# Seven products for eight in six of the eight up projections of a second MLP

## The chip, the cores and the metric

The kernel runs on one core of a Trainium2 chip. The metric is the device time of one execution in microseconds. The engines are named as in the profile: PE (TensorE), DVE (VectorE), ACT (ScalarE), POOL (GpSimd) and SP (SyncE, which here only starts transfers).

## What is computed

Two transformer blocks follow each other on 1024 rows of width 1024, in float32. The first has a token mixer and an MLP, the second a mixer, a cross-attention and an MLP. The change concerns the second MLP, which ends the program:

```python
def squared_relu_mlp(h, mlp_w1, mlp_w2):          # h 1024x1024, w1 1024x4096, w2 4096x1024
    hdn = square(relu(einsum('bld,df->blf', h, mlp_w1)))      # up projection
    return einsum('blf,fd->bld', hdn, mlp_w2)                 # down projection
h = layer_norm(ALPHA * h + squared_relu_mlp(h, mlp_w1, mlp_w2), ln3_g, ln3_b)
```

## The kernel before

Every float32 operand of a matmul is held as two float16 parts, hi and lo, with x = hi + lo; a product is three matmuls, hi·hi, hi·lo and lo·hi, accumulated in PSUM (`gemm`, L684 to L686). A matmul has 128 rows of weights loaded and streams 512 columns.

Each MLP is cut into NF = 8 chunks of 512 hidden features. PE does the up projection of chunk 0, then for u = 0 to 6 the up projection of chunk u + 1 and the down projection of chunk u, and at the end the down projection of chunk 7. In what follows up(u) and down(u) are these. An up projection is 8 jobs (`hidden_job`), one for each 128 features and 512 rows of tokens, of 8 blocks of K times 3 matmuls: 24 each, 192 in all. A down projection is 16 jobs (`down_job`) of 4 times 3 matmuls, also 192. Jobs take the PSUM banks 0 to 3 in turn; PE waits for semaphore `evac` of the bank.

Around PE the other engines work in orders that are written out by hand, one list for each engine:

- SP loads the next half chunk of weights (1 MB) into the staging buffer `WS` (two halves) as soon as POOL has freed it.
- ACT rounds `WS` to the hi part in `WB` (L1493) and scales `WS` (L1495); `WB` has two slots, which chunks use in turn. ACT also empties the banks of an up projection into `TMP`, a ring of four (L1462), and squares there (L1741).
- POOL forms the lo part of the weights, `WB` lo = `WS` - `WB` hi (L557), then drains and raises `w_split` (L560). At the start of the second MLP it has one more task between the weights of chunk 1 and those of down(0): `residual` (L610, L612), 16 operations on the rows `R`.
- DVE turns a square in `TMP` into hi and lo of the hidden matrix `H` (`split_piece`, a CAST L2084 and a TENSOR_TENSOR L2086, one such pair is called a piece). It is this CAST that raises `evac` and so frees the bank of an up job. A down job's bank is freed when DVE has added it to `R` (`gated_add`, L2442).

DVE takes pieces and additions in one fixed order: the 8 pieces of up(1), then the 16 additions of down(0), the 8 pieces of up(2), and so on.

Of the kernel before, what the change touches and what calls it, by code (L numbers as in the profile page):

```python
# [16 lines left out]
P = 128  # L17
SEQ = 1024
D = 1024
TT = SEQ // P  # L20
KT = D // P
HALF = 512
CHUNK = 64
EPS = 1e-5
# [94 lines left out]
def program(nc, I, out, block_decay):  # L119
    ctx = ExitStack()  # L120
    with ctx:
# [34 lines left out]
        w_split = sem("w_split")  # L156
        job_done = sem("job_done")
# [35 lines left out]
        NF = 4096 // HALF  # L193

# [4 lines left out]
        def deep(c):  # L199

            return WB[:, c % 2, :, :].rearrange("p l (k n) -> p l k n", k=4)
# [19 lines left out]
        N_ENGINES = 3  # L221

# [217 lines left out]
        def _(sp):  # L440
# [42 lines left out]
            def deep_chunk(c, src):  # L483

                for hf in range(2):
                    stage(c, hf, [(WS[:, hf, :].rearrange("p (k n) -> p k n", k=2),
                                   by_k(src)[:, 2 * hf:2 * hf + 2, :])])

            def mlp_stream(c0, w1, w2):
                wide_chunk(c0, [(w1, 0, HALF)])  # L490
                with sp.Fori(0, NF - 1) as j:
                    for hf in range(2):
                        sp.wait_ge(w_stage_free, 2 * (c0 + 1) + hf + 1 + 4 * j)
                        sp.dma_start(WS[:, hf, :].rearrange("p (k n) -> p k n", k=4),
                                     by_k(w1)[:, 4 * hf:4 * hf + 4, bass.ds((j + 1) * HALF, HALF)]
                                     ).then_inc(w_loaded[hf], 16)
                    for hf in range(2):
                        sp.wait_ge(w_stage_free, 2 * (c0 + 2) + hf + 1 + 4 * j)
                        sp.dma_start(WS[:, hf, :].rearrange("p (k n) -> p k n", k=2),
                                     by_k(w2)[:, bass.ds(4 * j + 2 * hf, 2), :]).then_inc(w_loaded[hf], 16)  # L500
                deep_chunk(c0 + 2 * NF - 1, w2[(NF - 1) * HALF:NF * HALF, :])

# [15 lines left out]
            mlp_stream(C["mlp1"], w_ff1, w_ff2)  # L518
# [15 lines left out]
            mlp_stream(C["mlp2"], w1_2, w2_2)  # L534
# [13 lines left out]
        def _(pool):  # L548
# [12 lines left out]

            def gate_columns(c, n):
# [9 lines left out]
            def gate_rows(c, i=0):  # L572

                row = S[:, 12, :].rearrange("p (a n) -> p a n", a=1).to_broadcast([P, 2, D])
                for hf in range(2):
                    pool.wait_ge(w_loaded[hf], loaded_at[c] + 32 * i)
                    w = WS[:, hf, :].rearrange("p (k n) -> p k n", k=2)
                    pool.tensor_tensor(w, w, row, ALU.mult)
                    pool.drain().then_inc(w_gated, 1)

            def split_narrow(c, width):
                n = 4 * width
                for hf in range(2):
                    pool.wait_ge(w_hi, 2 * c + 1 + hf)
# [31 lines left out]
            while c < N_CHUNKS:  # L616
                if c in (C["mlp1"], C["mlp2"]):
                    for u in range(2):
                        split((c + u) % 2, 2 * (c + u) + 1, 4)
                    if c == C["mlp2"]:  # L620
                        residual(2, "wo", 0)
                    gated = c == C["mlp1"]
                    with pool.Fori(0, NF - 1 - gated) as j:
                        for u in range(2):
                            split((c + u) % 2, 2 * (c + u) + 5 + 4 * j)
                    if gated:
                        split(c % 2, 2 * (c + 14) + 1)
                        need_wide(pool, LATE_JOBS[6])
                        need_wide(pool, LATE_JOBS[7])
                        gate_rows(c + 15)  # L630
                        split((c + 15) % 2, 2 * (c + 15) + 1)
# [6 lines left out]
                else:  # L638
                    split(c % 2, 2 * c + 1, 4)
# [15 lines left out]
        used_jobs = []  # L655


        @block.tensor
        def _(pe):
# [387 lines left out]
            def mlp(c0, src, last, rest_at):  # L1047
# [8 lines left out]
                def down_job(W, j, par):  # L1056
# [2004 lines left out]
```

## Time and profile before

| | |
|---|---|
| median of 3 runs | 2814.84 us (2813.55 to 2815.96) |
| span of the profiled execution | 2814.4 us |
| second MLP in it, from its first up job to the end | about 2149 to 2814 us |

The profile is of one execution; the page gives its span, and its device time is not given apart. Start times in the rows are microseconds from the start of the span. A matmul's own duration overlaps with the next one's, so the pace of PE is read from the distance between starts.

### The profile page before, as it was taken

The numbers are of one execution on the slowest core, as the hardware profiler recorded it, in microseconds if no ns is written. First come the engines' busy times: TensorE is split into PE (matmuls) and PEld (weight loads), VectorE is DVE, ScalarE is ACT, GpSimd is POOL, SyncE is SP. The second block draws the span as 40 slices with busy tenths as digits, with TensorE's granted clock in tenths as the row PEclk, the third lists the DMA queues.
The fourth block names the chain that finished last, engine by engine and source line by source line (L and its number), as shares of the span: only waits on it lengthen the run. The fifth ranks groups of instructions, "written<-read, shape, count | busy, mean of one in ns | idle before, by whom it ended". The sixth has DMA issues, their size and how long they took to land.

```text
span 2814.4 us, 33977 instructions
## 1 busy us (share of the span) xinstructions
PE 2653.3 (94%) x13340; PEld 1368.6 (49%) x13340; DVE 1435.5 (51%) x2294; ACT 966.3 (34%) x1154; POOL 686.1 (24%) x355
## 2 busy tenths in 40 slices
PE   6999999888999999999978899888999999999998
PEld 3677766444444444444454444344544444444443
DVE  6255344565744444675675749654336622222225
ACT  3434315035223332334244353253425332332231
POOL 1212024012212212321542231126013621221222
PEclk9999999999999999999989999999999999999999
DMA  7311131202111101221021230110001111110111
GB/s 302 117 60 68 43 120 46 90 30 90 54 37 60 60 30 60 75 96 40 31 90 66 70 116 30 45 44 32 31 30 60 60 42 49 60 60 31 60 45 60
DMA packets 55590, 182.44 MB, mean 65 GB/s; under 512 B 3952, under 2 KB 4368, under 8 KB 48016
## 3 DMA queue, kind: packets, MB, share of 16 engines
q1 hardware_dynamic: 47136, 138.89, 14.5%
q10 hardware_dynamic: 8304, 41.46, 4.0%
q8 instruction: 105, 1.72, 0.3%
q14 instruction: 45, 0.37, 0.0%
HBM read 170.90 MB, written 9.45 MB: 64 GB/s over the span
## 4 chain that ended last, share of the span: by engine, by line
PE 77%; DVE 9%; ACT 4%; POOLq 3%; DVEq 3%; issue 2%; POOL 1%; DMA 1%; ACTq 1%; SPq 0%
PE PS L684 23%; PE PS L685 23%; PE PS L686 23%; POOLq L613 1%; DVE XT L2086 1%; POOLq L611 1%; PE PS L723 1%; PE PS L1426 1%; POOL WB L557 1%; DVEq L2085 1%; PE PS L1399 1%; ACT WB L1493 1%; ACT WS L1495 1%; PE PS L972 1%; DMA Hf<-in_w_ada 1%
## 5 line engine op out<-in xcount | busy, mean ns | idle before, releaser
L557 POOL TENSOR_TENSOR WB<-WS,WB 128x512 f16<-128x512 f32 (+1 forms) x264 | 488.1, 1881 | 1854.4 <-ACT WS L1495 1854.1
L684 PE MATMUL PS<-XT,WB 128*128 128x512 f16 x1568 | 597.7, 381 | 10.5 <-DVE Hf L2084 5.3
L685 PE MATMUL PS<-XT,WB 128*128 128x512 f16 x1568 | 597.8, 381 | 0.0
L686 PE MATMUL PS<-XT,WB 128*128 128x512 f16 x1568 | 597.0, 381 | 0.0
L684 PE MATMUL PS<-WB,Hf 128*128 128x512 f16 x1440 | 551.5, 383 | 21.1 <-DVE Hf L2086 5.1
L685 PE MATMUL PS<-WB,Hf 128*128 128x512 f16 x1440 | 550.7, 382 | 0.0
L686 PE MATMUL PS<-WB,Hf 128*128 128x512 f16 x1440 | 550.3, 382 | 0.0
L2084 DVE CAST Hf<-S 128x512 f16<-128x512 f32 x172 | 148.8, 865 | 490.2 <-ACT S L1741 385.5
L1493 ACT ACTIVATE WB<-WS 128x2048 f16<-128x2048 f32 (+3 forms) x118 | 212.5, 1801 | 506.3 <-PE PS L686 471.1
L2442 DVE SCALAR_TENSOR_TENSOR R<-PS,R 128x512 f32<-128x512 f32 x208 | 143.0, 691 | 258.9 <-PE PS L686 251.8
L684 PEld LDWEIGHTS PS<-XT,WB 128*128 128x128 f16 x1568 | 154.2, 98 | 196.4 <-DVE XT L2086 5.5
L686 PEld LDWEIGHTS PS<-XT,WB 128*128 128x128 f16 x1568 | 154.1, 98 | 187.1 <-issue 3.8
L685 PEld LDWEIGHTS PS<-XT,WB 128*128 128x128 f16 x1568 | 154.0, 98 | 184.4 <-issue 3.1
L684 PEld LDWEIGHTS PS<-WB,Hf 128*128 128x128 f16 x1440 | 142.1, 99 | 198.6 <-issue 13.2
L686 PEld LDWEIGHTS PS<-WB,Hf 128*128 128x128 f16 x1440 | 142.0, 99 | 173.4 <-issue 6.3
L685 PEld LDWEIGHTS PS<-WB,Hf 128*128 128x128 f16 x1440 | 142.1, 99 | 172.8 <-issue 7.8
L1462 ACT ACTIVATE S<-PS 128x512 f32<-128x512 f32 x148 | 87.6, 594 | 393.5 <-PE PS L686 368.5
L1495 ACT ACTIVATE WS<-WS 128x2048 f32<-128x2048 f32 (+3 forms) x118 | 212.0, 1797 | 0.0
L684 PE MATMUL PS<-WB,XT 128*128 128x256 f16 (+2 forms) x640 | 169.0, 273 | 3.8 <-POOLq L588 2.3
L685 PE MATMUL PS<-WB,XT 128*128 128x256 f16 (+2 forms) x640 | 168.9, 273 | 0.0
L686 PE MATMUL PS<-WB,XT 128*128 128x256 f16 (+2 forms) x640 | 168.9, 273 | 0.0
L2086 DVE TENSOR_TENSOR Hf<-S,Hf 128x512 f16<-128x512 f32 x172 | 160.0, 930 | 16.2 <-issue 0.4
(381 smaller groups left out, 2744.2 us busy)
## 6 DMA issues: line engine op xcount, KB each, us to landing
WS<-in_w_ff SPq DMA_DIRECT2D x32, 1024.0 KB, 5.1
WS<-in_mlp_w SPq DMA_DIRECT2D x32, 1024.0 KB, 5.2
WS<-in_w_mix SPq DMA_DIRECT2D x20, 1024.0 KB, 4.9
Hf<-in_w_ada ACTq DMA_DIRECT2D x12, 1024.0 KB, 5.8
Hf<-in_w_ada SPq DMA_DIRECT2D x8, 1024.0 KB, 10.9
WS<-in_w_out SPq DMA_DIRECT2D x8, 1024.0 KB, 5.1
R<-in_x SPq DMA_DIRECT2D x4, 1024.0 KB, 9.9
R<-in_x ACTq DMA_DIRECT2D x2, 2048.0 KB, 7.9
```

Of the source, the lines that this page charges most:

```text
L557: op = pool.tensor_tensor(WB[:, slot, 1, at:at + n], WS[:, hf, i * n:(i + 1) * n], WB[:, slot, 0, at:at + n], ALU.subtract)
L611: pool.drain()
L613: pool.drain().then_inc(res_ready, 1)
L684: pe.matmul(o, ah, bh, start=(first and k == 0), stop=False, skip_group_check=True)
L685: pe.matmul(o, ah, bl, start=False, stop=False, skip_group_check=True)
L686: mm = pe.matmul(o, al, bh, start=False, stop=(last and k == n - 1), skip_group_check=True)
L1462: return act.activation(TMP[:, q % 4, :], src, func, scale=scale, bias=bias)
L1493: act.activation(rank_pair(hf, 0) if n == 64 else WB[:, slot, 0, hf * n:(hf + 1) * n], WS[:, hf, 0:n], ACT.Copy, scale=W_SCALE)
L1495: act.activation(WS[:, hf, 0:n], WS[:, hf, 0:n], ACT.Copy, scale=W_SCALE).then_inc(w_hi, 1)
L2084: dve.tensor_copy(hi, TMP[:, q % 4, :]).then_inc(evac[bank], 1)
L2086: dve.tensor_tensor(lo, TMP[:, q % 4, :], hi, ALU.subtract).then_inc(piece_done, 1)
L2442: dve.scalar_tensor_tensor(r, PS[:, b, :], 1 / (W_SCALE * scale * (ALPHA if first else 1.0)), r, ALU.mult, ALU.add).then_inc(evac[b], 1)
```

## The change

`FAST` names the chunks 2 to 7 of the second MLP. For these the up projection is done in half blocks: the 1024 of K and the 512 features of a weight chunk are cut into q11, q12, q21, q22 (512 by 256 each), the 1024x1024 activations into a11, a12, a21, a22 (512 by 512), and the four blocks of the result are formed from seven products of sums and differences (`PRODUCTS`) in place of eight products. Each product is 2 groups (256 features are 2 times 128) of 4 blocks of K times 3 matmuls.

- The sums of activation blocks s1 to s4 are formed once, by DVE, in `corner_sums(j)`: a call after each of the 8 pieces of up(1). They live in `S` as hi and lo.
- The differences of weight blocks t1 to t4 are formed by POOL for every fast chunk (`form_sums`), in place in `WS`. ACT rounds each of the seven forms to hi and POOL forms each lo (`split_forms`).
- The products use banks 4 to 7. ACT copies intermediate ones to `kept`, DVE adds them (`product_sum`) into `TMP`, ACT squares, DVE splits (`split_hidden`).
- PE does six products of up(u), the first two jobs of down(u - 1), the seventh product, and the other 14 jobs.
- In both MLPs the loops of ACT, POOL, DVE and SP are written out, a down chunk is staged and split by halves of its output columns, and PE starts a down projection when the half it needs is there (`w_half`), all jobs of one half first.

The core of the diff:

```diff
 
...
+        FORM_INDEX = {"q11": 0, "q21": 1, "q22": 2, "t1": 3, "t2": 4, "t3": 5, "t4": 6}
+        FORM_HI = {"q11": 1, "q21": 2, "t1": 3, "q22": 2, "t2": 4, "t3": 5, "t4": 6}
+        QUAD_AT = {"q11": (0, 0), "t3": (0, 0), "t1": (0, 1), "q12": (0, 1), "q21": (1, 0), "t4": (1, 0),
+                   "q22": (1, 1), "t2": (1, 1)}
...
+        def form_at(m, u, form, l):
+
+            i, a = FORM_INDEX[form], fast_slot(m, u)
+            slot, i = (a, i) if i < 4 else (1 - a, i - 4)
+            return WB[:, slot, l, i * 1024:(i + 1) * 1024].rearrange("p (k n) -> p k n", k=4)
+        KEPT_UNITS = {"mlp2": (11, 12)}
+
...
+            def split_down(m, u, gated=False):
+
+                c, slot = down_chunk(m, u), down_slot(m, u)
+                for hf in range(2):
+                    pool.wait_ge(w_hi, hi_count(c) + 1 + hf)
+                    n = slice(hf * 2048, (hf + 1) * 2048)
...
+            def split_forms(m, u):
+
+                at = FAST_BASE[m] + u - 2
+
+                def form_sums(forms):
+
+                    for form in forms:
+                        out, a, b = {"t1": ("q12", "q12", "q11"), "t2": ("q22", "q22", "t1"), "t3": ("q11", "t2", "q11"),
+                                     "t4": ("q21", "q21", "t2")}[form]
+                        pool.tensor_tensor(quad_stage(out), quad_stage(a), quad_stage(b), ALU.subtract)
+                        pool.drain().then_inc(form_sum, 1)
+
+                for form in FORM_INDEX:
+                    if form == "q21":
+                        form_sums(("t1",))
+                    if form == "t1":
+                        form_sums(("t2",))
+                    if form == "t2":
+                        form_sums(("t3", "t4"))
+                    pool.wait_ge(form_hi, 6 * at + FORM_HI[form])
+                    pool.tensor_tensor(form_at(m, u, form, 1), quad_stage(form), form_at(m, u, form, 0), ALU.subtract)
+                    pool.drain().then_inc(form_lo, 1)
+                    if form in ("t3", "t4"):
...
+                        if u in FAST[m]:
+                            split_forms(m, u)
+                        elif u > 1:
...
+                def fast_product(u, i):
+
+                    at = FAST_BASE[m] + u - 2
+                    form, rows, bank = PRODUCTS[i]
+                    pe.wait_ge(form_lo, 7 * at + FORM_INDEX[form] + 1)
+                    for f in range(2):
+                        if form == "q21" and at:
+                            pe.wait_ge(up_sum, 6 * (at - 1) + 3 + f)
+                        if form == "q11" and at:
+                            pe.wait_ge(up_last, 2 * (at - 1) + 1 + f)
+                        if form == "t1":
+                            pe.wait_ge(up_kept, 6 * at + 1 + f)
+                        if form == "t2":
+                            pe.wait_ge(up_sum, 6 * at + 1 + f)
+                        if form == "q22":
+                            pe.wait_ge(up_kept, 6 * at + 3 + f)
+                        if form == "t3":
+                            pe.wait_ge(up_kept, 6 * at + 5 + f)
+                        if form == "t4":
+                            pe.wait_ge(up_sum, 6 * at + 5 + f)
+                        c = slice(f * P, (f + 1) * P)
+                        gemm(PS[:, 4 + bank + f, :], lambda k: tuple(form_at(m, u, form, l)[:, k, c] for l in range(2)),
+                             lambda k: tuple(sum_rows(m, rows, l, k) if rows in SIGN_UNITS[m] else
+                                             block_rows(rows, l, k) for l in range(2)), 4,
+                             first=form in ("q21", "q11", "t1")).then_inc(up_done, 1)
 
...
+
+                    c = up_chunk(m, u)
+                    if u in fast:
+                        if u == fast[0]:
+                            for k in range(K[0] - 4, K[0]):
+                                need_side(pe, k)
+                            pe.wait_ge(corner_sum, 4 * (1 + (m == "mlp2" and len(FAST["mlp1"]) > 0)))
...
-                    pe.wait_ge(piece_done, q0 + 8 * (u + 1))
+                    down_at[m, u - 1] = J[0]
+                    pe.wait_ge(piece_done, q0 + 8 * u)
                     for j in range(16):
-                        down_job(deep(c + 1), j, u % 2)
+                        if j % 8 == 0:
+                            need_half(u - 1, j // 8)
+                        down_job(u - 1, j % 8, j // 8)
+                        if j == 1 and u in fast:
+                            fast_product(u, 6)
                     chunk_used()
-
...
+                def up_forms(u):
+
+                    c, at = up_chunk(m, u), FAST_BASE[m] + u - 2
+                    if u == fast[0]:
+                        act.wait_ge(job_done, used_jobs[up_chunk(m, u - 1)])
+                    else:
+                        act.wait_ge(up_done, 14 * at)
+                    for hf, forms in enumerate((("q11",), ("q21", "q22"))):
+                        act.wait_ge(w_loaded[hf], loaded_at[c])
+                        for form in forms:
+                            act.activation(form_at(m, u, form, 0), quad_stage(form), ACT.Copy, scale=W_SCALE)
+                        act.drain()
+                        act.activation(WS[:, hf, :], WS[:, hf, :], ACT.Copy, scale=W_SCALE).then_inc(form_hi, 1)
+                    act.wait_ge(form_sum, 4 * at + 1)
+                    form_round(u, "t1").then_inc(form_hi, 1)
+                    act.wait_ge(job_done, down_at[m, u - 2] + 8)
+                    act.wait_ge(form_sum, 4 * at + 2)
+                    form_round(u, "t2").then_inc(form_hi, 1)
+                    act.wait_ge(form_sum, 4 * at + 3)
+                    form_round(u, "t3").then_inc(form_hi, 1)
+
+                def last_form(u):
+
+                    at = FAST_BASE[m] + u - 2
+                    act.wait_ge(job_done, down_at[m, u - 2] + 16)
+                    act.wait_ge(form_sum, 4 * at + 4)
+                    form_round(u, "t4").then_inc(form_hi, 1)
+
...
+                        act.wait_ge(up_sum, 6 * at + n + 1)
+                        act.activation(TMP[:, q % 4, :], TMP[:, q % 4, :], ACT.Relu, scale=UNSCALE * F_SCALE ** 0.5)
+                        act.drain()
+                        act.activation(TMP[:, q % 4, :], TMP[:, q % 4, :], ACT.Square).then_inc(tmp_full, 1)
+
+                    if at:
+                        act.wait_ge(up_sum, 6 * at)
+                    for f in range(2):
+                        keep(0, f, f)
+                    squared(0)
+                    round_down(u - 1, 0)
+                    keep(1, 4, 0)
+                    squared(1)
+                    keep(1, 5, 1)
+                    for f in range(2):
+                        keep(0, 6 + f, f)
+                    round_down(u - 1, 1)
+                    for n in range(2, 6):
+                        squared(n)
+                    for f in range(2):
+                        act.wait_ge(up_done, 14 * at + 13 + f)
+                        q = Q[0]
+                        to_tmp(PS[:, 6 + f, :], ACT.Relu, scale=UNSCALE * F_SCALE ** 0.5).then_inc(up_last, 1)
...
+                def product_sum(u, n):
+
+                    at, f = FAST_BASE[m] + u - 2, n % 2
+                    bank, i, job, copy = ((4, 0, 2, 1), (4, 0, 8, 5), (6, 1, 10, 3))[n // 2]
+                    if n < 2:
+                        bank = 6
+                    dve.wait_ge(up_kept, 6 * at + copy + f)
+                    dve.wait_ge(up_done, 14 * at + job + f + 1)
+                    dve.drain()
+                    dve.tensor_tensor(TMP[:, (Q[0] + n - 2 * (n >= 2)) % 4, :], PS[:, bank + f, :], kept(m, i, f),
+                                      ALU.add).then_inc(up_sum, 1)
+
+                def corner_sums(j):
+
+                    k = j // 2
+                    a11, a12, x, y = kept(m, 0, 0), kept(m, 0, 1), kept(m, 1, 0), kept(m, 1, 1)
+
+                    def joined(dst, name):
+                        dve.tensor_tensor(dst, block_rows(name, 0, k), block_rows(name, 1, k), ALU.add)
+
+                    def parts(name, x):
+                        dve.drain()
+                        dve.tensor_copy(sum_rows(m, name, 0, k), x)
+                        dve.drain()
+                        return dve.tensor_tensor(sum_rows(m, name, 1, k), x, sum_rows(m, name, 0, k), ALU.subtract)
+
+                    if j % 2 == 0:
+                        joined(x, "a21")
+                        joined(y, "a22")
+                        joined(a11, "a11")
+                        joined(a12, "a12")
+                        dve.drain()
+                        dve.tensor_tensor(y, x, y, ALU.add)
+                        dve.tensor_tensor(x, a11, x, ALU.subtract)
+                        parts("s1", y)
+                    else:
+                        parts("s3", x)
+                        dve.drain()
+                        dve.tensor_tensor(y, y, a11, ALU.subtract)
+                        dve.drain()
+                        dve.tensor_tensor(a12, a12, y, ALU.subtract)
+                        parts("s2", y)
+                        parts("s4", a12)
...
-                hidden(1, 0, None if last else s5_steps)
-                down(0, False)
+                for u in range(NF):
+                    if u in fast:
+                        for n in range(2):
+                            product_sum(u, n)
+                        for n in range(2):
+                            split_hidden(u, n)
+                        for n in range(2, 6):
+                            product_sum(u, n)
+                        for n in range(2, 6):
+                            split_hidden(u, n)
+                    elif u == 1 and fast:
+                        hidden(u, corner_sums)
+                    else:
+                        hidden(u, None if last else {0: s5_setup, 1: s5_folds, NF - 1: s5_steps}.get(u))
```

What a built program of each kernel has on an engine shows the same. On DVE, this stands at the start of the second MLP, where the pieces of up(0) end and those of up(1) follow (Hf is `H`). Before:

```order
L2084 CAST Hf<-S 128x512 [waits tmp_full]
L2086 TENSOR_TENSOR Hf<-S,Hf 128x512
L2083 REGISTER_ALU
L2084 CAST Hf<-S 128x512 [waits tmp_full]
L2086 TENSOR_TENSOR Hf<-S,Hf 128x512
```

Now, from the first piece of up(1) to the second one and the operations behind it:

```order
L2316 CAST Hf<-S 128x512 [waits tmp_full]
L2318 TENSOR_TENSOR Hf<-S,Hf 128x512
L2759 TENSOR_TENSOR S<-XT 128x512 x4
L2773 TENSOR_TENSOR S<-S 128x512
L2774 TENSOR_TENSOR S<-S 128x512
L2763 CAST S<-S 128x512
L2765 TENSOR_TENSOR S<-S 128x512
L2316 CAST Hf<-S 128x512 [waits tmp_full]
L2318 TENSOR_TENSOR Hf<-S,Hf 128x512
L2763 CAST S<-S 128x512
L2765 TENSOR_TENSOR S<-S 128x512
L2779 TENSOR_TENSOR S<-S 128x512
```

Between two pieces of up(1) there are now eight operations of `corner_sums`, 64 in all, and the additions of down(0) stand behind all of them.

On POOL, the end of `residual` is followed before by the loop over the splits:

```order
L612 TENSOR_TENSOR R<-R,S 128x1024
L623 UNCONDITIONAL_BRANCH
L623 ISA
L557 TENSOR_TENSOR WB<-WS,WB 128x2048 [waits w_hi]
```

and now by the split of down(0), all of the forms of chunk 2, and the split of down(1):

```order
L707 TENSOR_TENSOR R<-R,S 128x1024
L625 TENSOR_TENSOR WB<-WS,WB 128x2048 [waits w_hi] x2
L650 TENSOR_TENSOR WB<-WS,WB 128x1024 [waits form_hi]
L639 TENSOR_TENSOR WS<-WS 128x4x256
L650 TENSOR_TENSOR WB<-WS,WB 128x1024 [waits form_hi] x2
L639 TENSOR_TENSOR WS<-WS 128x4x256
L650 TENSOR_TENSOR WB<-WS,WB 128x1024 [waits form_hi]
L639 TENSOR_TENSOR WS<-WS 128x4x256 x2
L650 TENSOR_TENSOR WB<-WS,WB 128x1024 [waits form_hi] x3
L625 TENSOR_TENSOR WB<-WS,WB 128x2048 [waits w_hi] x2
```

A chunk's up weights thus cost POOL 11 operations of half the size in place of 2.

## Rows read from the trace of the kernel before

**Rows 1.** The page: busy time of the engines and share of the span.

```profile
PE 2653.3 (94%) x13340; PEld 1368.6 (49%) x13340; DVE 1435.5 (51%) x2294; ACT 966.3 (34%) x1154; POOL 686.1 (24%) x355
```

**Rows 2.** PE's waits from 2150 to 2815 us: us in total, times, longest.

```profile
PE PS L684 <- POOLq L560: 3.8, 1, 3.8
```

**Rows 3.** Busy us in stretches, in the page's order of engines; then granted clock, DMA.

```profile
2220.00:2240.00 20.00, 16.17 (x68) 6.95 (x68) 9.35 (x9) 8.65 (x6) 12.05 (x3) 0.91 0.55 172
2267.15:2350.03 82.88, 82.88 (x386) 37.59 (x384) 23.16 (x32) 24.21 (x24) 16.23 (x4) 1.00 0.16 51
```

**Rows 4.** Timeline of PE: start, us; end of up(1), start of down(0), up(2).

```profile
2219.59 0.38 PE L685 MATMUL PS<-XT,WB 128*128 128x512 f16 x1
2219.80 0.38 PE L686 MATMUL PS<-XT,WB 128*128 128x512 f16 x1
2224.01 0.49 PE L684 MATMUL PS<-WB,Hf 128*128 128x512 f16 x1 [3.83 <-POOLq L560]
...
2227.65 0.38 PE L684 MATMUL PS<-WB,Hf 128*128 128x512 f16 x1
...
2267.15 0.38 PE L684 MATMUL PS<-XT,WB 128*128 128x512 f16 x1
```

**Rows 5.** Timeline of DVE: pieces of up(1), from the first to the last.

```profile
2188.49 0.43 DVE L2084 CAST Hf<-S 128x512 f16<-128x512 f32 x1 [4.61 <-ACT S L1741]
2189.01 2.69 DVE L2086 TENSOR_TENSOR Hf<-S,Hf 128x512 f16<-128x512 f32 x1
2191.61 2.56 DVE L2084 CAST Hf<-S 128x512 f16<-128x512 f32 x1
2194.27 2.70 DVE L2086 TENSOR_TENSOR Hf<-S,Hf 128x512 f16<-128x512 f32 x1
...
2212.76 2.57 DVE L2084 CAST Hf<-S 128x512 f16<-128x512 f32 x1
2215.42 4.55 DVE L2086 TENSOR_TENSOR Hf<-S,Hf 128x512 f16<-128x512 f32 x1
2219.89 4.28 DVE L2084 CAST Hf<-S 128x512 f16<-128x512 f32 x1
2224.26 0.69 DVE L2086 TENSOR_TENSOR Hf<-S,Hf 128x512 f16<-128x512 f32 x1
2224.87 0.42 DVE L2084 CAST Hf<-S 128x512 f16<-128x512 f32 x1
2225.38 0.69 DVE L2086 TENSOR_TENSOR Hf<-S,Hf 128x512 f16<-128x512 f32 x1
```

**Rows 6.** Timeline of POOL in that stretch, and a split without DVE beside it.

```profile
2212.43 2.61 POOL L612 TENSOR_TENSOR R<-R,S 128x1024 f32<-128x1024 f32 x1
2215.35 8.54 POOL L557 TENSOR_TENSOR WB<-WS,WB 128x2048 f16<-128x2048 f32 x2 [0.31 <-issue]
2228.64 4.08 POOL L557 TENSOR_TENSOR WB<-WS,WB 128x2048 f16<-128x2048 f32 x1 [4.75 <-ACT WS L1495]
```

**Rows 7.** Groups of POOL by form: busy, mean ns of one, idle before.

```profile
L612 POOL TENSOR_TENSOR R<-R,S 128x1024 f32<-128x1024 f32 x24 | 59.2, 2465 | 3.5
L587 POOL TENSOR_TENSOR WB<-WS,WB 128x1024 f16<-128x1024 f32 x6 | 13.6, 2296 | 79.5 <-ACT WS L1495 79.5
```

**Rows 8.** Timeline of DVE while POOL is idle, the last three with a drain.

```profile
2121.08 0.42 DVE L2084 CAST XT<-S 128x512 f16<-128x512 f32 x1
2121.59 0.69 DVE L2086 TENSOR_TENSOR XT<-S,XT 128x512 f16<-128x512 f32 x1
2122.20 0.42 DVE L2084 CAST XT<-S 128x512 f16<-128x512 f32 x1
...
1735.89 0.69 DVE L2893 TENSOR_TENSOR S<-S 128x512 f32<-128x512 f32 x1
1736.65 0.69 DVE L2895 TENSOR_TENSOR S<-S 128x512 f32<-128x512 f32 x1
```

**Rows 9.** Timeline of ACT: a half chunk rounded and scaled, a bank emptied and squared.

```profile
2267.43 1.91 ACT L1493 ACTIVATE WB<-WS 128x2048 f16<-128x2048 f32 x1 [34.30 <-PE PS L686]
2269.24 1.89 ACT L1495 ACTIVATE WS<-WS 128x2048 f32<-128x2048 f32 x1
2277.79 0.60 ACT L1462 ACTIVATE S<-PS 128x512 f32<-128x512 f32 x1 [1.87 <-PE PS L686]
2278.45 0.63 ACT L1741 ACTIVATE S<-S 128x512 f32<-128x512 f32 x1
```

**Rows 10.** Timeline of DVE and of SP: an addition of down(0); a chunk's two transfers.

```profile
2228.50 0.69 DVE L2442 SCALAR_TENSOR_TENSOR R<-PS,R 128x512 f32<-128x512 f32 x1 [2.42 <-PE PS L686]
...
2275.48 4.39 SPq L494 DMA_DIRECT2D WS<-in_mlp_w  x2
```

More of the change, by code:

```diff
@@ L156, in program @@
         w_split = sem("w_split")
+        w_half = sem("w_half")
+        form_hi, form_lo, form_sum = sem("form_hi"), sem("form_lo"), sem("form_sum")
+        sums_in = sem("sums_in")
+        up_done, up_kept, up_sum, up_last = sem("up_done"), sem("up_kept"), sem("up_sum"), sem("up_last")
+        corner_sum = sem("corner_sum")
         job_done = sem("job_done")
@@ L1045, in _, with mlp @@
             pieces += 16
-            def mlp(c0, src, last, rest_at):
+            def mlp(m, src, last, rest_at):
+                c0, fast = C[m], FAST[m]
                 def hidden_job(W, j):
@@ L1433, in _ @@
             pieces += 16
[L1434 removed]
+            mlp("mlp2", None, True, 2)
         @block.scalar
@@ L1726, in _, with mlp, hidden @@
                       second=False)
-            def mlp(c0, name, lnw, lnb, last):
-                def hidden(extra_j, extra_q, setup=None, first=False):
+            def mlp(m, name, lnw, lnb, last):
+                c0, fast = C[m], FAST[m]
+                def hidden(setup=None, first=False):
                     for i in range(8):
@@ new lines, in round_down, with form_round @@
+                def round_down(u, hf, gated=None):
+                    c = down_chunk(m, u)
+                    if gated is not None:
+                        act.wait_ge(w_gated, gated + hf)
+                    down_free(u, hf)
+                    round_half(down_slot(m, u), hf, 2048, loaded_at[c], None)
+                def form_round(u, form):
+                    return act.activation(form_at(m, u, form, 0), quad_stage(form), ACT.Copy)
+                def up_forms(u):
[17 more added lines that the diff above has]
+                    form_round(u, "t3").then_inc(form_hi, 1)
@@ L2482, in _, with mlp, hidden @@
             J[0] += 2 * TT
-            def mlp(gate, par, last):
-                def hidden(par_, extra_q, setup=None):
+            def mlp(m, gate, par, last):
+                fast = FAST[m]
+                def hidden(u, setup=None):
                     for j in range(8):
@@ L2496, in down @@
+                def down(u, tail, between=None):
                     for j in range(16):
@@ L2512, in mlp, with between @@
-                with dve.Fori(0, 3 if last else 2) as i:
-                    for u in range(2):
-                        hidden((u + 1) % 2, 16 * i)
-                        if last and u == 0:
-                            dve.wait_ge(res_ready, 24)
-                        down(48 * i, False)
-                J[0] += 96 if last else 48
-                Q[0] += 32 if last else 16
-                hidden(1, 0, None if last else s5_steps)
-                down(0, False)
+                for u in range(NF):
+                    if u in fast:
+                        for n in range(2):
[8 more added lines that the diff above has]
+                        hidden(u, corner_sums)
+                    else:
+                        hidden(u, None if last else {0: s5_setup, 1: s5_folds, NF - 1: s5_steps}.get(u))
+                    if u == 0:
+                        continue
+                    if u == 1 and last:
+                        dve.wait_ge(res_ready, 24)
+                    def between(j):
+                        if u in fast and j in (1, 2):
+                            split_hidden(u, 5 + j)
+                    down(u - 1, False, between)
```

238 lines of the change are left out of this document (146 added, 92 removed).

## The prediction

> **What bounds the kernel now.** I read the page first: PE is busy 94% of the span, no other engine over 51% [rows 1]. Then PE's waits inside the second MLP: there is a single one, of 3.8 us, ended by POOL [rows 2]. Then stretches by time: a chunk pair (up and down) takes 82.88 us in which PE never idles, at the full granted clock [rows 3]; it holds 384 matmuls, so 0.2158 us each, which is also the distance between two starts [rows 4]. So from 2267.15 on PE sets the end, and every matmul that goes is worth 0.216 us as long as no wait appears. The start of this MLP is another matter. From 2191.6 to 2226.1 us DVE has no gap: its CASTs and TENSOR_TENSORs take 2.6 us instead of 0.42 and 0.69 [rows 5, 8], each ending just after an operation of POOL, whose `residual` runs without a pause until 2215.0 and is followed by 8.5 us of splits [rows 6]. PE does not feel this, since nothing waits closely for those pieces: DVE's last piece of up(1) ends at 2226.07 [rows 5], two us before the first addition of down(0) at 2228.50 [rows 10] has its bank.
>
> **What is removed.** A fast chunk has 7 products of 24 matmuls, 168 for 192. Six chunks save 144 matmuls: 144 x 0.2158 = **31.1 us**, at the full clock and with no new wait.
>
> **What the fast chunks add, and why it hides.** I lay out one chunk from T, the start of its first product. A group of 12 matmuls is 2.59 us, a product 5.18, the chunk 30 groups or 77.7 us. Prices: an ACT rounding or scaling of a half chunk 1.9, a bank emptied 0.60, a squaring pass 0.63 [rows 9]; 1024 columns on ACT by interpolation between 512 and 2048 about 1.0; a POOL lo part of 1024 columns 2.3, a difference in float32 2.5 [rows 7], a split of a half 4.1 [rows 6]; both transfers of a chunk 4.4 [rows 10].
> - Forms of the next chunk: ACT is through with this chunk at about T+43.4 and rounds and scales the two halves until T+50.4. POOL takes from T+46.4 eight operations, about 20 us, then t2 and t3 (ACT may round them once the first half of the down jobs is done, T+57), until T+71. PE asks for them at T+78 and later; t4 is ready at T+81 and is used at T+114.
> - Down weights: the first half of `WS` is free at T-7, loaded well before T, rounded by ACT behind the second product (T+14), split by POOL at T+18.5. PE needs it at T+31. The second is at T+34, needed at T+57.
> - Banks 4 to 7: each is copied or added (0.6 to 0.7) while PE works one product, 5.2 us, in another pair. DVE's additions read PSUM and one SBUF tensor, a kind that takes 0.69 even beside POOL (the addition at 2228.50 beside the split at 2228.64) [rows 6, 10]. The seventh product needs its sums at T+36.3, they are there at T+31.8.
> The smallest slack is thus 4.5 us. POOL is busy about 36 of 77.7 us, ACT about 45. I cost all this at nothing; if a cover is gone, a chunk pays the lateness, six times.
>
> **Halves and written-out loops.** PE now starts down(0) with POOL's first half split. It was done at about 2219.6, half of the 8.5 us [rows 6], and PE was ready at 2220.0 [rows 4]. So the 3.8 us wait would go, and the eight half-speed matmuls behind it too (2224.01 to 2227.65 for 8 matmuls and a bit; granted clock 0.91 in that stretch, that is some time at 1.2 in place of 2.4 GHz [rows 3, 4]), 1.7 us more. But a later stall comes in its place, next. The first MLP has no such wait; its engines have the same work in the same order, and I cost it at nothing.
>
> **What corner_sums costs, the term that decides.** It puts 64 DVE operations of 128x512 between the pieces of up(1). Without POOL beside them: after a TENSOR_TENSOR the next starts 0.61 us later, 0.76 with a drain between; after a CAST 0.51 [rows 8]. An even call is 3 x 0.61 + 0.76 + 0.61 + 0.76 + 0.51 + 0.61 = 5.1, an odd one 5.6. Four of each: **42.9 us**, 0.67 an operation. All of them come on top, since DVE had no gap there. While `residual` and the split of down(0) last, DVE gets one operation for each of POOL's, whatever it is; before, the thirteen of 2188.5 to 2224.3 were all of pieces, now four are and nine are sums. The total of what comes behind is the same.
>
> Then POOL comes back while DVE is still at it: ACT ends its squares of up(1) when PE has done job 7. PE's jobs 5, 6, 7 wait for DVE (they need the CASTs of pieces 1, 2, 3, at 2215.3, 2229.7 and 2236), job 7 ends near 2242, so ACT starts the forms of chunk 2 near 2243 and POOL near 2246. Eight POOL operations follow without a wait (the ninth needs eight down jobs, which don't exist yet). Against each, one DVE operation takes about 2.56 for 0.67 [rows 5]: 8 x 1.9 = **15.1 us** more. This has two ends. None blocked gives 0. More than eight can't be blocked there, so 15.1 is near the top; I take 15.1, since every operation of up(1)'s pieces behaves so wherever POOL runs [rows 5].
>
> This is where a rule of the Trainium skill speaks against the change. Its page SBUF — State Buffer, section SBUF: two separate sides, says that VectorE and GpSimd share a port pair as an exclusive lock held for the whole instruction, by a VectorE operation with two SBUF inputs or in a two-port mode against GpSimd; the other fully blocks. The trace agrees with 2.70 for 0.69 us. The rows have no operation with two float16 inputs; by the rule those of `joined` block as well.
>
> DVE would end piece 7 and its sums at 2226.07 + 42.9 + 15.1 = 2284.1. Down jobs 0 to 3 of down(0) get their banks from pieces 4 to 7, but job 4 needs the first addition, and that stands behind everything: 2284.1 + 0.17 + 0.69 = 2284.9. PE then has 12 jobs, 31.1 us, with the first eight matmuls at half speed after the stall, 1.7: up(2) starts at 2317.7. Before, 2267.15 [rows 4]. That is **+50.5 us**, in which the 3.8 + 1.7 of before are already counted as gone.
>
> **The sum.** 50.5 - 31.1 = +19.4 us: a span of 2814.4 + 19.4 = 2833.8. The profiled span lies 0.4 under the median of the runs, 2814.84, so a run should take about **2834 us**.
>
> **Rivals.**
> 1. *POOL doesn't catch DVE in its sums* (it starts later, or DVE slips several operations through a gap between two of POOL's). The 15.1 falls away: up(2) starts at 2302.6, +4.3 net, 2819 us. For it: POOL's start depends on a chain of ACT and PE that I placed only to a few us. Against it: in the 32 us of `residual` DVE never got two through [rows 5]. A partial form, half of the eight, gives 2827.
> 2. *Faster.* The sums are cheap enough for PE's lead over DVE. Job 4 of down(0) could start at 2230.4 without any stall; the change breaks even when DVE ends 19.4 us earlier than in my sum, at 2264.7 rather than 2284.1. One mechanism does it: the lock spares the sums, because operations on `XT` and `S` alone aren't blocked by POOL, in `residual` either. Then DVE does the sums, 42.9, and eight pieces at 1.12, 9.0, straight from 2188.5 and ends at 2240.4; job 4 starts at 2241.3, up(2) 32.8 later at 2274.1, 6.9 behind 2267.15, and the result is 2814.8 + 6.9 - 31.1 = 2791 (some us more for pieces that stay blocked). Against it: two-input operations on `S` and `Hf` are blocked in [rows 5], and nothing in the rows sets `XT` apart.
> 3. *The sixteen additions of hi and lo run at twice the pace*, 0.27 us less each, 4.3 in all: 2830, inside my range. They read float16 and write float32.
> 4. *The fast chunks stall too.* POOL's or ACT's chain is longer than laid out, or DVE's CASTs, held by a POOL that is now busy half the time, are late for the seventh product. At 2 us a chunk the time is 2846; if each chunk loses its whole 5.18 the time is 2865. For it: the 4.5 us of slack is small. Against it: most chains have over 12.
>
> On rival 3, the page VectorE: DVE Perf Modes of the Trainium skill, section What auto-detection actually checks, gives the double pace of a two-input operation only where every tensor is 16-bit. By that rule the sum stays at 2834; no row here has such an operation.
>
> **How the numbers follow.** A measurement of this kernel can tell about 0.2%, 5.6 us, from no change: 2809.2 to 2820.5 is "same". My forecast, with its partial forms and rival 3 (2825 to 2842): 0.70. Rival 1 in full, around 2819, falls on both sides of that bound: 0.10. Rival 2: 0.09. Rival 4: 0.11. So faster 0.10, same 0.09, slower 0.81. The range 2816 to 2846 takes in rival 1, and rival 4 in its mild form; outside stay rival 2 and the strong form of 4, under 2 in 10.
>
> **What the profile would show.** If I am right: PE waits for DVE at jobs 5 to 7 of up(1) and at jobs 1 to 4 of down(0), some 50 us in all, the last ending at about 2285; DVE busy without a gap from 2188 to 2286, with durations near 2.6 us until 2224 and again from about 2246 to 2266; up(2) starting near 2318; then six stretches of 77.7 us and PE without a wait to the end. If the eight aren't blocked, the durations between 2246 and 2266 are 0.4 to 0.7. If the lock spares the sums, DVE's operations are short before 2224 as well. If rival 4 holds, PE waits for `form_lo`, `w_half` or `up_sum` in each fast chunk. I am wrong altogether if PE has work that I don't see while DVE is at its sums, or if banks 4 to 7 tie a product to something later.

## The result, and the profile after

The changed kernel takes 2836.09 us (median of 4 runs, 2834.71 to 2837.59) against 2815.11 (4 runs, 2813.55 to 2815.96): a ratio of 1.0072, 95% interval 1.0059 to 1.0085. It is 21 us slower (17 to 24 by the interval). The forecast was 2834 us, and slower had been given 0.81. The profiled execution has a span of 2832.9 us, and its device time, 2834.71 us, is 1.8 us more.

The page of the changed kernel, busy time by engine, answers to [rows 1]:

```profile
PE 2631.5 (93%) x13196; PEld 1359.5 (48%) x13196; DVE 1519.7 (54%) x2394; ACT 1007.9 (36%) x1220; POOL 784.5 (28%) x409
```

PE has the 144 matmuls less (13340 to 13196), and still ends later. Its busy time falls by 22 us and not by the 31.1 that 144 matmuls take, since some 50 matmuls now run at half speed behind the waits shown next. The view of its waits in the second MLP (us in total, times, longest), where [rows 2] had one row of 3.8 us:

```profile
PE PS L783 <- DVE Hf L2316: 40.4, 6, 11.7
PE PS L783 <- DVE R L2674: 4.6, 1, 4.6
```

The wait for POOL is gone, and DVE is the new releaser, first with the CASTs that free up banks (L2316), at last with the first addition of down(0) (L2674). PE's timeline where the long waits end, and up(2):

```profile
2212.94 0.61 PE L783 MATMUL PS<-XT,WB 128*128 128x512 f16 x1 [9.19 <-DVE Hf L2316]
2229.03 0.61 PE L783 MATMUL PS<-XT,WB 128*128 128x512 f16 x1 [9.05 <-DVE Hf L2316]
2253.75 0.61 PE L783 MATMUL PS<-WB,Hf 128*128 128x512 f16 x1 [9.04 <-DVE Hf L2316]
2269.93 0.61 PE L783 MATMUL PS<-WB,Hf 128*128 128x512 f16 x1 [11.65 <-DVE Hf L2316]
2283.45 0.61 PE L783 MATMUL PS<-WB,Hf 128*128 128x512 f16 x1 [4.60 <-DVE R L2674]
2316.80 0.38 PE L783 MATMUL PS<-XT,WB 128*128 128x512 f16 x1
```

Up(2) starts at 2316.80 in place of 2267.15 [rows 4]: 49.65 us later. DVE's timeline shows what it did instead, over the same stretch as [rows 5]:

```profile
2187.59 0.43 DVE L2316 CAST Hf<-S 128x512 f16<-128x512 f32 x1 [4.60 <-ACT S L1885]
2188.11 2.69 DVE L2318 TENSOR_TENSOR Hf<-S,Hf 128x512 f16<-128x512 f32 x1
2190.72 8.95 DVE L2759 TENSOR_TENSOR S<-XT 128x512 f32<-128x512 f16 x4
2199.75 2.68 DVE L2773 TENSOR_TENSOR S<-S 128x512 f32<-128x512 f32 x1
...
2229.67 2.49 DVE L2759 TENSOR_TENSOR S<-XT 128x512 f32<-128x512 f16 x4
2232.24 0.69 DVE L2773 TENSOR_TENSOR S<-S 128x512 f32<-128x512 f32 x1
...
2246.45 2.19 DVE L2763 CAST S<-S 128x512 f16<-128x512 f32 x1
2248.72 2.71 DVE L2765 TENSOR_TENSOR S<-S 128x512 f16<-128x512 f32 x1
...
2281.83 0.69 DVE L2765 TENSOR_TENSOR S<-S 128x512 f16<-128x512 f32 x1
2282.70 3.04 DVE L2674 SCALAR_TENSOR_TENSOR R<-PS,R 128x512 f32<-128x512 f32 x4 [0.18 <-issue]
```

The same four additions of `joined` take 2.49 us when POOL rests and 8.95 beside `residual`. The second slow stretch, from 2246.45 on, begins with POOL's forms of chunk 2 (POOL's timeline: the first two and the last of the eight that follow each other, then the ninth):

```profile
2246.06 2.30 POOL L650 TENSOR_TENSOR WB<-WS,WB 128x1024 f16<-128x1024 f32 x1 [22.25 <-ACT WS L1924]
2248.54 2.34 POOL L639 TENSOR_TENSOR WS<-WS 128x1024 f32<-128x1024 f32 x1 [0.18 <-issue]
...
2263.68 2.57 POOL L639 TENSOR_TENSOR WS<-WS 128x1024 f32<-128x1024 f32 x1 [0.18 <-issue]
2297.42 2.13 POOL L650 TENSOR_TENSOR WB<-WS,WB 128x1024 f16<-128x1024 f32 x1 [31.17 <-ACT WB L1910]
```

And in stretches, with the columns of [rows 3]: the time of the stalls, then two of the six fast chunks.

```profile
2260.00:2280.00 20.00, 7.72 (x24) 2.74 (x24) 18.65 (x24) 0.00 (x0) 5.89 (x3) 0.66 0.00 0
2316.30:2394.00 77.70, 77.70 (x362) 35.24 (x360) 27.72 (x38) 31.12 (x35) 32.46 (x13) 1.00 0.17 55
2549.50:2627.30 77.80, 77.80 (x362) 35.31 (x361) 27.72 (x38) 31.12 (x35) 32.48 (x13) 1.00 0.17 55
```

A fast chunk takes 77.7 us at the full granted clock where a plain one took 82.88 [rows 3]. From the start of up(2) to the end of the span it is 516.1 us now (2832.9 - 2316.8) and 547.25 before (2814.4 - 2267.15). So the seven products give 31.15 us, and all of the loss lies ahead of them.

The executions differ by some us before they come to the changed part, so a second measure is of use: the time from one and the same matmul to the end of the span. I take PE's first matmul behind its last transposes (`PS<-BASE`). In both kernels 14 jobs of up projections lie between it and down(0). Up(0) itself begins two jobs earlier, at 2131.35 in the trace of before, and not at 2149 as the table of the kernel before has it. Before, and in the changed kernel:

```profile
2147.50 0.38 PE L684 MATMUL PS<-XT,WB 128*128 128x512 f16 x1
```

```profile
2146.60 0.38 PE L783 MATMUL PS<-XT,WB 128*128 128x512 f16 x1
```

From there to the end it is 666.9 us before (2814.4 - 2147.5) and 686.3 now (2832.9 - 2146.6), 19.4 us more. The table below gives the same measure for the experiments.

### The profile page after: what moved, and what is told of

The parts are those of the page before. It is cut to its first block, busy times and chain, and to the rows that moved or that the text cites. A ratio compares the mean times of both kernels' runs of the same rounds, so it can differ in the third digit from the quotient of the medians.

```text
span 2832.9 us, 33523 instructions
## 1 busy us (share of the span) xinstructions
PE 2631.5 (93%) x13196; PEld 1359.5 (48%) x13196; DVE 1519.7 (54%) x2394; ACT 1007.9 (36%) x1220; POOL 784.5 (28%) x409
## 4 chain that ended last, share of the span: by engine, by line
PE 77%; DVE 11%; ACT 4%; DVEq 3%; issue 2%; POOLq 1%; DMA 1%; ACTq 1%; POOL 0%; SPq 0%
PE PS L783 23%; PE PS L784 22%; PE PS L785 22%; PE PS L822 1%; DVE XT L2318 1%; PE PS L1567 1%; DVEq L2317 1%; DVE Hf L2318 1%; ACT WB L1634 1%; PE PS L1540 1%; DVE S L2765 1%; ACT WS L1636 1%; PE PS L1071 1%; POOLq L708 1%; DMA Hf<-in_w_ada 1%
## 5 line engine op out<-in xcount | busy, mean ns | idle before, releaser
L614 POOL TENSOR_TENSOR WB<-WS,WB 128x512 f16<-128x512 f32 (+1 forms) x220 | 308.1, 1433 | 1221.5 <-ACT WS L1636 1221.5
L783 PE MATMUL PS<-XT,WB 128*128 128x512 f16 x1328 | 508.5, 383 | 28.9 <-DVE Hf L2316 23.5
L784 PE MATMUL PS<-XT,WB 128*128 128x512 f16 x1328 | 508.2, 383 | 0.0
L785 PE MATMUL PS<-XT,WB 128*128 128x512 f16 x1328 | 507.1, 382 | 0.0
L1634 ACT ACTIVATE WB<-WS 128x2048 f16<-128x2048 f32 (+3 forms) x106 | 189.9, 1791 | 332.9 <-PE PS L785 302.0
L2674 DVE SCALAR_TENSOR_TENSOR R<-PS,R 128x512 f32<-128x512 f32 x208 | 143.0, 691 | 240.4 <-PE PS L785 231.8
L2316 DVE CAST Hf<-S 128x512 f16<-128x512 f32 x124 | 99.7, 804 | 302.1 <-ACT S L1885 196.5
L625 POOL TENSOR_TENSOR WB<-WS,WB 128x2048 f16<-128x2048 f32 x32 | 131.1, 4098 | 374.8 <-ACT WS L1636 372.7
L783 PEld LDWEIGHTS PS<-XT,WB 128*128 128x128 f16 x1328 | 130.9, 99 | 188.2 <-DVE Hf L2316 19.2
L785 PEld LDWEIGHTS PS<-XT,WB 128*128 128x128 f16 x1328 | 131.0, 99 | 159.9 <-issue 5.8
L784 PEld LDWEIGHTS PS<-XT,WB 128*128 128x128 f16 x1328 | 130.9, 99 | 156.2 <-issue 4.1
L1636 ACT ACTIVATE WS<-WS 128x2048 f32<-128x2048 f32 (+3 forms) x106 | 189.2, 1785 | 0.0
L1603 ACT ACTIVATE S<-PS 128x512 f32<-128x512 f32 x112 | 66.2, 594 | 298.4 <-PE PS L785 273.5
## 6 DMA issues: line engine op xcount, KB each, us to landing
Hf<-in_w_ada SPq DMA_DIRECT2D x8, 1024.0 KB, 10.6
```

Of the source, the lines that this page charges most:

```text
L614: op = pool.tensor_tensor(WB[:, slot, 1, at:at + n], WS[:, hf, i * n:(i + 1) * n], WB[:, slot, 0, at:at + n], ALU.subtract)
L625: pool.tensor_tensor(WB[:, slot, 1, n], WS[:, hf, :], WB[:, slot, 0, n], ALU.subtract).then_inc(w_stage_free, 1)
L783: pe.matmul(o, ah, bh, start=(first and k == 0), stop=False, skip_group_check=True)
L784: pe.matmul(o, ah, bl, start=False, stop=False, skip_group_check=True)
L785: mm = pe.matmul(o, al, bh, start=False, stop=(last and k == n - 1), skip_group_check=True)
L1603: return act.activation(TMP[:, q % 4, :], src, func, scale=scale, bias=bias)
```

## The experiments

The ratios are against the kernel before on the same chip. The kernel before ran at a median of 2816.45 us beside e1 to e4 and 2816.33 beside e5 and e6, so ratios are compared rather than times. A ratio has an interval of some us. The traces are finer, one execution each: this is the time from the matmul named above to the end of the span, against the 666.9 us of the kernel before.

| | that matmul starts | to the end | against before | expected |
|---|---|---|---|---|
| the change | 2146.60 | 686.3 | +19.4 | +19.4 |
| e1 | 2151.45 | 661.3 | -5.6 | -5.5 |
| e2 | 2149.87 | 670.2 | +3.3 | +4.4 |
| e3 | 2146.66 | 656.3 | -10.6 | -31 |
| e4 | 2150.05 | 668.7 | +1.8 | +2 |
| e5 | 2148.03 | 635.4 | -31.5 | -30.7 |
| e6 | 2152.90 | 707.9 | +41.0 | +40.4 |

For e2 and e6, whose expectations are told against the changed kernel (15 us less, 21 more), the last column adds its 19.4. The second column shows that the executions reach this matmul up to 6 us apart, whatever the version.

**e1: no fast chunk.** Only the written-out loops and the halves stay.

```diff
-        FAST = {"mlp1": range(0), "mlp2": range(2, NF)}
+        FAST = {"mlp1": range(0), "mlp2": range(0)}
```

> No fast chunk at all: what is left of the change is the written-out loops and the down weights by halves. My theory: these alone are worth the 3.8 us wait at the start of down(0) and the 1.7 us of half-speed matmuls behind it, so about 2809.5 us and PE without a wait from 2150 us on. Rival: the longer programs of ACT, DVE and POOL or the transfers with shorter rows cost something of their own, and part of the +21 us of the whole change is here: then 2815 us or more.

Measured: 2811.47 us, ratio 0.9983 (0.9973 to 0.9992), 4.8 us faster. PE has no wait from `residual` to the end; what the view lists from 2130 us on is ahead of the MLP. My theory's 5.5 us lies within the interval (2.3 to 7.6), and the trace is nearer to it: 5.6 us less from the matmul above to the end. The rival, a cost of the longer programs, falls. The 49.65 us are therefore not in this part.

**e2: POOL's forms of chunk 2 wait for the sums.**

```diff
                 at = FAST_BASE[m] + u - 2
+                if at == 0:
+                    pool.wait_ge(corner_sum, 4)
 
                 def form_sums(forms):
```

> The changed kernel, but POOL starts the forms of chunk 2 only when DVE has finished corner_sums. My theory: the eight POOL operations that ran beside the sums held eight DVE operations for about 1.9 us each; without them the sums end near 2267, up(2) starts near 2302 in place of 2316.8, and the time is 15 us lower, about 2821 us. Rival: the sums cost what they cost by their number, and DVE's long durations only name an idle time that something else sets: then up(2) starts where it did, 2836 us. Second rival: the forms now come late for the first products, and PE waits for form_lo: the gain is part of 15 us.

Measured: 2820.37 us, ratio 1.0013 (1.0004 to 1.0022). Against the 1.0072 of the change that is 16.6 us less (4.5 either way by the two intervals), where I expected 15. Its timeline of DVE behind 2246 has no long duration, and the one of POOL shows its first form after the sums:

```profile
2190.86 0.43 DVE L2318 CAST Hf<-S 128x512 f16<-128x512 f32 x1 [4.61 <-ACT S L1887]
...
2251.35 0.69 DVE L2320 TENSOR_TENSOR Hf<-S,Hf 128x512 f16<-128x512 f32 x1
2252.13 0.43 DVE L2765 CAST S<-S 128x512 f16<-128x512 f32 x1
...
2269.89 0.69 DVE L2767 TENSOR_TENSOR S<-S 128x512 f16<-128x512 f32 x1
2270.77 3.04 DVE L2676 SCALAR_TENSOR_TENSOR R<-PS,R 128x512 f32<-128x512 f32 x4 [0.18 <-issue]
```

```profile
2270.70 2.12 POOL L652 TENSOR_TENSOR WB<-WS,WB 128x1024 f16<-128x1024 f32 x1 [43.61 <-DVEq L2786]
```

Adding a wait to POOL made the kernel faster. DVE's instructions are the same in both; only what POOL did beside them differs. From the first CAST of up(1) to the last sum DVE took 79.7 us here (2270.58 - 2190.86) and 94.9 in the changed kernel (2282.52 - 2187.59): 15.2 us less. That is the part of the loss in which POOL's operations hold DVE's. The waits of PE are all for DVE, none for `form_lo`, so the second rival falls too.

**e3: five fast chunks, the sums between the additions of down(0) and down(1).** The helper functions for slots and counts are moved by one chunk as well, since FAST now begins at 3.

```diff
-        FAST = {"mlp1": range(0), "mlp2": range(2, NF)}
+        FAST = {"mlp1": range(0), "mlp2": range(3, NF)}
...
-                    elif u == 1 and fast:
-                        hidden(u, corner_sums)
...
                         if u in fast and j in (1, 2):
                             split_hidden(u, 5 + j)
+                        if last and u in (1, 2) and j % 4 == 1:
+                            corner_sums(4 * (u - 1) + j // 4)
```

> Fast chunks 3 to 7 (five), and corner_sums taken out of the pieces of up(1): one of its eight calls behind every fourth addition of down(0) and down(1), where DVE has 1.9 us free per addition. My theory: a call (5.1 to 5.6 us) and four additions (3.5) fit in the 10.4 us that PE takes for four jobs, and PE is four banks ahead, so nothing stalls: 2815.1 - 5.5 - 5 x 5.18 = 2784 us. Rival: POOL's splits, which fall into the same stretches, hold the sums so long that PE runs out of banks: some us in each of down(0) and down(1), 2790 us or more.

Measured: 2806.39 us, ratio 0.9965 (0.9951 to 0.9979): 9.9 us faster than before, not 31. My expectation missed by 21 us, on the side of its rival. PE's waits:

```profile
PE PS L785 <- DVE R L2676: 15.7, 2, 10.7
PE PS L785 <- DVEq L2786: 1.2, 1, 1.2
```

The two waits for an addition are behind the first call in each of down(0) and down(1). With the third they make 16.9 us, and the half-speed matmuls behind the two add some 3.6, which is the 21 us missed. The one in down(1), on DVE and on POOL:

```profile
2315.06 9.02 DVE L2761 TENSOR_TENSOR S<-XT 128x512 f32<-128x512 f16 x4
2324.16 2.67 DVE L2775 TENSOR_TENSOR S<-S 128x512 f32<-128x512 f32 x1
```

```profile
2315.88 2.59 POOL L641 TENSOR_TENSOR WS<-WS 128x1024 f32<-128x1024 f32 x1 [0.18 <-issue]
```

A call that I had priced at 5.1 us took 19.6 (2315.06 to 2334.6), since it ran beside POOL's forms of chunk 3, which began at 2313.57. The other calls of down(1) ran nearly all beside an idle POOL, and PE's only further wait, at the start of up(3), is the one of 1.2 us. I had made the same mistake as the change: room on DVE counted without asking what POOL does then.

**e4: six fast chunks, all sums in down(0).**

```diff
-                    elif u == 1 and fast:
-                        hidden(u, corner_sums)
...
+                        if last and u == 1 and j % 2 == 1:
+                            corner_sums(j // 2)
```

> Six fast chunks as in the change, but the eight calls of corner_sums stand behind every second addition of down(0), none in the pieces of up(1). My theory: DVE has 16 x 0.78 + 42.9 us to do there and is held eight times by POOL's forms (15.1), 70.5 us from about 2225.5, so PE starts up(2) near 2297 in place of 2316.8: about 2817 us. Rival: the forms of chunk 2 now start earlier and the lock costs less, or DVE uses gaps better than counted: 2805 us.

Measured: 2819.82 us, ratio 1.0010 (1.0001 to 1.0019), some 3 us over the kernel before; expected was +2. PE starts up(2) when the sums are done:

```profile
2300.06 0.59 PE L783 MATMUL PS<-XT,WB 128*128 128x512 f16 x1 [15.46 <-DVEq L2784]
```

That is 3 us behind the 2297 I gave, but this execution also came to the second MLP 3.4 us later than that of the changed kernel (table), and `residual` ended 2.9 us later (2218.0 against 2215.1). From its first addition, 2228.50, to the last sum, 2299.78, DVE took 71.3 us; I had 70.5. The additions leave DVE 30 us in a down projection, and the sums need 43 and more.

**e5: as e3, the calls where POOL rests.**

```diff
...
-                    elif u == 1 and fast:
-                        hidden(u, corner_sums)
+                    elif u == 2 and fast:
+                        hidden(u, lambda j: corner_sums({1: 5, 3: 6, 5: 7}[j]) if j in (1, 3, 5) else None)
...
+                        if last and u == 1 and j in (6, 8, 10, 12, 15):
+                            corner_sums((6, 8, 10, 12, 15).index(j))
```

> As e3 (five fast chunks, 3 to 7), but the eight calls stand only where POOL is idle in e3's trace: five behind additions 6, 8, 10, 12 and 15 of down(0), three behind pieces 1, 3 and 5 of up(2). My theory: e3 lost its gain to the lock (its first and fifth call ran beside POOL's splits and forms, 2.6 us an operation), so the same work at these places stalls nothing: 4.8 us for the halves and 5 x 5.18 for the products under the kernel before, about 2785 us, and no wait of PE over 1 us from 2150 us on. Rival: it is the length of a call, 5 us and more in front of the additions, that runs PE out of banks wherever it stands: then the waits of 5 and 11 us stay, and the time is 2800 us or more.

Measured: 2784.87 us, ratio 0.9884 (0.9867 to 0.99): 32.7 us faster than before (28 to 37). Expected were 2785 us, that is 30.7 less. PE has no wait in the second MLP behind its transposes. Its stretch of down(0) and up(2), and its first fast chunk:

```profile
2215.00:2298.00 83.00, 83.00 (x386) 37.56 (x385) 69.19 (x91) 24.44 (x24) 25.89 (x7) 1.00 0.24 77
2298.00:2376.00 78.00, 78.00 (x363) 35.31 (x361) 24.82 (x35) 27.59 (x30) 29.57 (x13) 1.00 0.13 41
```

DVE is busy for 69 of 83 us and PE for all 83. The 64 operations are those of e3; only their place differs, and 21 to 22 us with it (2806.39 and 2784.87 us; 656.3 and 635.4 in the table). The call length as such is no limit. One of the five calls in down(0) still met a split of POOL:

```profile
2267.51 8.87 DVE L2761 TENSOR_TENSOR S<-XT 128x512 f32<-128x512 f16 x4
```

It came behind the last addition, with nothing of PE waiting on it. This version is faster than both kernels.

**e6: each even call twice,** in the changed kernel. The values are the same.

```diff
-                    if j % 2 == 0:
+                    for again in range(2 if j % 2 == 0 else 0):
                         joined(x, "a21")
...
                         parts("s1", y)
+                        dve.drain()
...
```

> The changed kernel with the eight operations of each even call of corner_sums done twice: 32 more DVE operations, the same values. My theory: DVE has no gap there, so the unblocked 5.1 to 5.3 us of each added copy come on top, except the first, which runs beside residual at 2.6 us an operation: 8 x 2.6 + 3 x 5.3 = 37 us at most, and at least 21 us if the blocked time only moves to other operations; POOL's own stretches are of fixed length, so I expect the lower one, 21 us: about 2857 us. Rival: PE's lead or some other engine sets the start of up(2) and part of the copies is hidden: under 2850 us.

Measured: 2857.41 us, ratio 1.0143 (1.0126 to 1.016), 0.0071 over the change, 20 us (6 either way). PE's waits for DVE are now

```profile
PE PS L783 <- DVE Hf L2316: 63.5, 5, 24.3
PE PS L783 <- DVE R L2674: 2.6, 1, 2.6
```

DVE's first CAST of up(1) and its last sum in this trace:

```profile
2193.89 0.43 DVE L2316 CAST Hf<-S 128x512 f16<-128x512 f32 x1 [4.60 <-ACT S L1885]
...
2309.98 0.69 DVE L2765 TENSOR_TENSOR S<-S 128x512 f16<-128x512 f32 x1
```

That is 116.8 us (2310.67 - 2193.89) where the changed kernel took 94.9: 21.9 us for 32 operations, 0.68 each, near the unblocked price, and nothing of it is hidden. Four unblocked copies of 5.2 us (2246.82 to 2252.02) are 20.8 of it, so the blocked time grew by about 1 us at most: it belongs to POOL's stretches, which hardly change their length with what DVE has in its queue.

## Why the prediction was right, point by point

- **Products.** 31.1 us forecast, 31.15 measured from the start of up(2) to the end. The chunk of 77.7 us came out, and PE has no wait in any of the six, so the covers that I costed at nothing held. Two sizes in them were off, on the safe side: POOL is busy 32.5 us in a chunk (I had about 36) and ACT 31.1 (I had about 45). The sums for the seventh product were there 32.1 us after the chunk's start (2348.90 - 2316.80), 31.8 forecast.
- **corner_sums, unblocked part.** 42.9 us forecast, 0.67 an operation. e6 gives 0.68 in its trace and 0.63 by the ratios.
- **The part held by POOL.** 15.1 us forecast; e2 takes it away, and DVE's stretch is 15.2 us shorter, the time 16.6. POOL's eight operations began at 2246.06, where I had 2246, and eight of DVE's were long, from the CAST at 2246.45 on.
- **The two together.** From the first CAST of up(1) to the end of DVE's work before down(0) it was 37.6 us (2226.07 - 2188.49) [rows 5] and is 94.9 (2282.52 - 2187.59): 57.3 more, 58.0 forecast. The 0.7 is one operation that slipped through beside `residual` (last section).
- **Start of up(2).** 2317.7 forecast, 2316.80 measured. That it is so close is in part luck, for small errors cancel: DVE's first piece of up(1) began 0.9 us earlier than in the execution of before, DVE's stretch was 0.7 shorter, and the 12 jobs behind the last wait took 33.35 us (2316.80 - 2283.45) where I had 32.8, since ten matmuls and not eight ran at half speed.
- **PE's waits.** Some 50 us forecast, the last ending at about 2285; 45.0 measured, the last ending at 2283.45.
- **Halves and loops.** 5.5 us forecast, 5.6 in e1's trace, 4.8 by its ratio.
- **The four banks of lead.** PE waited at jobs 5 and 6 of up(1) and at jobs 1, 2, 3 and 4 of down(0), as forecast from `evac`. At job 7 of up(1), where I had a wait too, it didn't wait, and at job 0 of down(0) only 0.24 us.
- **What was off.** The median lies 2 us over my time, while the part from the second MLP on came out at the 19.4 us forecast. The device time is 1.8 us over the span, not the 0.4 that I took from before. The other three runs had spans of 2834.3 to 2835.8; there is no trace of them, and the traces that there are reach the second MLP up to 6 us apart. What sets that spread stays open.
- **A reading that was thin.** I took it from the addition at 2228.50 that an operation with one PSUM and one SBUF input isn't held by POOL; but that one began before the split at 2228.64 [rows 6, 10]. The next one of before lies wholly inside that split, and shows it:

```profile
2231.09 0.69 DVE L2442 SCALAR_TENSOR_TENSOR R<-PS,R 128x512 f32<-128x512 f32 x1 [1.90 <-PE PS L686]
```

- **Rivals.** 1 (POOL doesn't meet the sums) is what e2 builds by force: I gave it 2819 and e2 is at 1.0013, which is 2818.8. 2 (the lock spares operations on `XT` and `S`) falls by the row of 8.95 us. 3 (the additions of two float16 parts at twice the pace) falls too: four of them take 2.49 us, 0.60 apart, like float32 ones (2232.24 and 2232.84 in the changed kernel). 4 (the fast chunks stall) falls by the stretches.

The rule of the page SBUF — State Buffer of the Trainium skill that I weighed, section SBUF: two separate sides, is borne out for operands that the rows of before lacked, two float16 inputs: 8.95 us for 2.49. The double pace that the page VectorE: DVE Perf Modes of the Trainium skill ties to all-16-bit operands in its section What auto-detection actually checks was not to be had with a float32 output, as it says; no run here has an all-16-bit one.

## What to carry to other kernels

A preparation that is done once costs its whole length if it stands in a queue that has no gap, and the place must be looked for in two timelines at once: the engine's own, and that of the engine whose operations hold it, here POOL. The same 64 operations cost some 55 us between the pieces of up(1) (the 49.65 by which up(2) starts later, and the 5.6 that the halves had gained), some 21 when four of the eight calls stand in each of down(0) and down(1) and two of them meet POOL, and nothing that can be measured where POOL rests. Before placing work on DVE, read what POOL does in those microseconds. Where POOL runs operations back to back, count a DVE operation with two SBUF inputs, and a CAST, at the length of one of POOL's (2.6 us here for 0.69 and 0.43); an addition that reads PSUM stayed at 0.69.

## What the runs showed of the hardware

- Four TENSOR_TENSORs without a drain between them do not cost four of POOL's operations. They took 8.95 and 9.02 us beside POOL, where four operations with a drain between most of them take about 10.6 (2199.75 to 2210.33). POOL's timeline of the changed kernel has one gap of 0.47 us there in place of 0.18. It looks as if two of them went through that gap; this was not tried. I had counted one for each.

```profile
2198.99 2.89 POOL L705 TENSOR_TENSOR R<-R,S 128x1024 f32<-128x1024 f32 x1 [0.47 <-issue]
```

- After each of the five stalls of 4.60 to 11.65 us in the changed kernel, PE's next eight to ten matmuls started 0.43 us apart, then 0.216 (2212.94 to 2216.58, and 2283.45 to 2287.69 and beyond), as after the single 3.8 us in [rows 4]. Such a stall costs 1.7 to 2.3 us on top of its length (8 to 11 times 0.21). The granted clock was 0.66 over the stretch 2260 to 2280, which has most of one. The stall of 1.20 us in the same stretch cost nothing more than itself: the full pace was there at once, although the stall of 11.65 us had ended only 6 us before. So it was after stalls of 1.24, 1.64 and 1.70 us in e4.

```profile
2276.09 0.39 PE L783 MATMUL PS<-WB,Hf 128*128 128x512 f16 x1 [1.20 <-DVE Hf L2316]
```

- These costs don't add up where another engine sets the pace. DVE's queue set when up(2) could start, so of the five only the half-speed matmuls behind the last stall, 2.3 us, moved it.
